# A four-layer decoder trunk on one core: stage boundaries with the last two output tiles in token halves, high terms first, and the second half's statistics between them

## The reference

```python
for i in range(DEPTH):
    ...
    hp = rmsnorm(xp, norm_g[i, 0])
    ...                                        # mp = mixer(hp), by i % 3
    xp = xp + rmsnorm(mp, norm_g[i, 1])
    ...
    xp = xp + rmsnorm(swiglu_ffn(rmsnorm(xp, norm_g[i, 2]), ffn_w1[i], ffn_w3[i], ffn_w2[i]), norm_g[i, 3])
```

## Time and profile before

| | us |
|---|---|
| median of three runs | 3369.45 |
| lowest and highest | 3368.85 and 3377.64 |
| the profiled execution | 3368.75 |
| its span in the trace | 3367.2 |

### The profile page before, as it was taken

One profiled execution on the slowest core, in us unless ns is written; L12 is line 12 of the kernel. 1 busy time (PEld: TensorE's weight loads), 2 busy tenths in 40 slices (PEclk: granted clock), 3 DMA queues, 4 the chain that ended last, 5 costly groups with the idle time before them and its releaser, 6 DMA issues.

```text
span 3367.2 us, 63399 instructions
## 1 busy us (share of the span) xinstructions
PE 3159.9 (94%) x26691; PEld 2913.2 (87%) x26691; DVE 1469.3 (44%) x2092; ACT 1078.8 (32%) x1529; POOL 170.6 (5%) x270
## 2 busy tenths in 40 slices
PE   7998999999999999899999899899999998899998
PEld 7986899999976666689999883789999896799998
DVE  3435644325460111254442599464432444554422
ACT  3413322222265444442222440432222332422222
POOL 1000100005000000010000100010000100100001
PEclk9998899999989999899999899899999898899999
DMA  4223223323205999822232220222332123222331
GB/s 112 82 63 107 69 87 87 101 76 78 79 29 203 362 390 389 296 70 87 87 98 84 62 69 0 64 71 87 87 99 76 57 75 111 71 82 87 94 95 45
DMA packets 472464, 368.12 MB, mean 109 GB/s; under 512 B 24745, under 2 KB 436830, under 8 KB 472316
## 3 DMA queue, kind: packets, MB, share of 16 engines
q1 hardware_dynamic: 459248, 349.25, 32.3%
q10 hardware_dynamic: 11020, 16.22, 1.4%
q0 software_dynamic: 2048, 0.53, 0.2%
HBM read 348.68 MB, written 17.26 MB: 109 GB/s over the span
## 4 chain that ended last, share of the span: by engine, by line
PE 80%; DVE 12%; ACT 4%; POOL 2%; issue 1%; ACTq 0%; POOLq 0%; DVEq 0%
PE acc L786 61%; PE acc L1274 3%; DVE big L2134 3%; PE acc L1243 2%; PE acc L1315 2%; PE acc L818 2%; DVE h_lo L1558 1%; POOL xT L766 1%; ACT mix L2567 1%; DVE wsp L1510 1%; DVE yT L1526 1%; PE acc L1047 1%; PE acc L1035 1%; DVE big L1586 1%; PE acc L1258 1%
## 5 line engine op out<-in xcount | busy, mean ns | idle before, releaser
L1510 DVE TENSOR_TENSOR wsp<-ring,wsp 128x1024 fp32r<-128x1024 f32 (+1 forms) x360 | 467.5, 1300 | 1122.9 <-ACT wsp L2217 1122.7
L786 PE MATMUL acc<-h_lo,wsp 128*128 128x272 f32 x4416 | 918.7, 290 | 0.0
L786 PE MATMUL acc<-h_hi,wsp 128*128 128x272 f32 x5376 | 897.6, 289 | 3.2 <-ACT rstd L2274 3.2
L2217 ACT ACTIVATE wsp<-ring 128x1024 fp32r<-128x1024 f32 (+1 forms) x360 | 401.6, 1117 | 1355.6 <-PE acc L786 1332.3
L786 PEld LDWEIGHTS acc<-h_hi,wsp 128*128 128x128 f32 x5376 | 758.9, 189 | 3.5 <-issue 3.5
L786 PEld LDWEIGHTS acc<-h_lo,wsp 128*128 128x128 f32 x4416 | 702.5, 191 | 0.0
L786 PE MATMUL acc<-i_hi,wsp 128*128 128x272 f32 x2560 | 440.4, 294 | 20.0 <-DVE wsp L1510 13.6
L786 PE MATMUL acc<-g_hi,wsp 128*128 128x272 f32 x2640 | 439.5, 288 | 0.0
L786 PEld LDWEIGHTS acc<-i_hi,wsp 128*128 128x128 f32 x2560 | 371.4, 194 | 22.8 <-issue 18.6
L786 PEld LDWEIGHTS acc<-g_hi,wsp 128*128 128x128 f32 x2640 | 371.7, 189 | 0.0
L786 PE MATMUL acc<-g_lo,wsp 128*128 128x272 f32 x1320 | 272.1, 288 | 0.0
(11 more groups left out here) (387 smaller groups left out, 3249.8 us busy)
## 6 DMA issues: line engine op xcount, KB each, us to landing
ring<-in_ffn_w SPq DMA_DIRECT2D x176, 512.0 KB, 3.9
mix<-in_cache_fox_v SPq DMA_DIRECT2D x96, 512.0 KB, 9.2
mix<-in_cache_fox_k SPq DMA_DIRECT2D x92, 512.0 KB, 8.8
ring<-in_ffn_w SPq DMA_DIRECT2D x64, 704.0 KB, 4.7
big<-in_cache_fox_k SPq DMA_DIRECT2D x32, 512.0 KB, 7.7
big<-in_cache_fox_v SPq DMA_DIRECT2D x32, 512.0 KB, 12.5
ring<-in_conv_w SPq DMA_DIRECT2D x24, 512.0 KB, 4.0
ring<-in_gla_wr SPq DMA_DIRECT2D x16, 512.0 KB, 4.0
```

The costliest lines, as they stand in the source:

```text
L786: last = pe.matmul(acc[:, bank + h, 0:HALF], wsp[:, s, w, k * P:(k + 1) * P], rhs[:, k0 + k, h * HALF:(h + 1) * HALF], start=start and k = ...
L1510: dve.tensor_tensor(wsp[:, s, 1, 0:tiles * P], ring[:, slot, 0:tiles * P], wsp[:, s, 0, 0:tiles * P], ALU.subtract).then_inc(wlo_done, 1)
L2217: act.activation(wsp[:, slot % SPLITS, 0, 0:tiles * P], ring[:, slot, 0:tiles * P], ACT.Copy)\
```

## The change

- The last two parts are computed half by half: for tokens 0 to 271 both parts, then for tokens 272 to 543 both. Behind a mixer the two parts are output tiles 6 and 7; in the ffn they are the two K blocks of tile 7. TensorE waits for the weights of both before the first.
- The column sums and the spread of half one stand inside the second half: the sums within its first part, the spread ahead of its second.
- Column sums and spread of half two go into the next stage's first tile, behind its first and its fourth high term.
- The first two tiles of a stage take all high terms (two products for each input tile) of both tiles, then the low terms of both, for half one, and then the same for half two.
- VectorE's order in `post` is new: the low part of the first weights goes behind three z of half one, and the z of half two alternate in pairs with the `h_lo` of half one. ScalarE makes the first two high parts of x early behind an ffn, and takes the root of half two behind the third.

```diff
@@ TensorE
-            def last_block(s, ktiles, k0, hi, lo, start, free):
+            def last_parts(parts, hi, lo, ready):
 
                 for h in range(2):
-                    for k in range(ktiles):
-                        if h == 1 and k == 4:
-                            pe.wait_ge(acc_out[4], free)
-                            column_sums(0)
...
+                    for i, (s, ktiles, k0, bank, first, last_one) in enumerate(parts):
+                        for k in range(ktiles):
+                            if h == 1 and i == 0 and k == 4:
+                                ready()
+                                column_sums(0)
+                            if h == 1 and i == 1 and k == 0:
+                                spread_half(0)
+                            for w, rhs in ((0, hi), (0, lo), (1, hi)):
+                                last = pe.matmul(acc[:, bank + h, 0:HALF], wsp[:, s, w, k * P:(k + 1) * P],
+                                                 rhs[:, k0 + k, HALVES[h]],
...
-            def post():
-
-                spread_half(0)
-                column_sums(1)
...
+            def second_sums(adds):
+
+                pe.wait_ge(acc_out[4], t.out[4])
+                column_sums(1, adds)
+                t.sum += adds
+
+            def second_spread():
+
                 spread_half(1)
                 t.out[4] += 1
...
+                for h in range(2):
+                    for j in range(2):
+                        if h == 0:
+                            pe.wait_ge(wlo_done, s0 + j + 1)
+                            pe.wait_ge(acc_out[2 * j], t.out[2 * j])
+                        for k in range(KD):
+                            if adds and h == 0 and j == 0:
+                                if k == 1:
+                                    second_sums(adds)
+                                if k == 4:
+                                    second_spread()
+                            high_terms(j, h, k)
+                    for j in range(2):
+                        last = low_terms(j, h)
+                        if h:
+                            last.then_inc(blk_done, 1)
...
                     else:
-                        last_block(j % SPLITS, KD, 0, o_hi, h_lo, True, o[4] + 2)
+                        pe.wait_ge(wlo_done, s0 + KD)
+                        pe.wait_ge(acc_out[6], o[6] + 1)
+                        t.early += 1
+                        last_parts(((0, KD, 0, 4, True, True), (1, KD, 0, 6, True, True)), o_hi, h_lo,
+                                   lambda: pe.wait_ge(early_out, t.early))
...
@@ VectorE
-                z_half(0, range(2))
+                z_half(0, range(3))
+                if mixer:
+                    dve.wait_ge(acc_out[4], t.out[4])
+                    add_square(squares, KD - 2, HALVES[1])
+                if weights:
+                    weights(0)
+                z_half(0, range(3, 5))
                 dve.wait_ge(last_sq, 2 * t.post + 2)
                 add_square(squares, KD - 1, HALVES[1])
-                z_half(0, range(2, 6))
+                z_half(0, range(5, KD))
                 dve.wait_ge(rcol_done, 2 * t.post + 2)
                 dve.reciprocal(rinv[:, 3:6], rcol[:, 3:6]).then_inc(rstd_done, 1)
-                z_half(0, range(6, KD))
-                between(1)
+                if lows:
+                    lows(0, range(2))
+                if weights:
+                    weights(1)
                 dve.wait_ge(spread_full, 2 * t.post + 2)
                 t.out[6] += 1
                 dve.wait_ge(acc_out[6], t.out[6])
-                z_half(1, range(2))
-                between(2)
-                z_half(1, range(2, KD))
+                for k in range(0, KD, 2):
+                    z_half(1, range(k, k + 2))
+                    if lows and k + 2 < KD:
+                        lows(0, range(k + 2, k + 4))
...
@@ ScalarE
+                if coming or mixer:
                     act.wait_ge(state_out, 16 * states[0])
                     high(0, KD, 16 * (t.blk // RING + 1), t.blk - 1)
...
+                if coming:
+                    for k in range(EARLY):
+                        high_half(*coming, 0, k)
+                act.wait_ge(blk_done, t.blk)
+                half_out(squares, bias, KD - 1, 1, last_sq, acc_out[6])
+                if coming or mixer:
+                    high(1, KD, 16 * (t.blk // RING + 1), t.blk)
...
+                        if early is not None and not h and k == 2:
+                            root_of(1)
+                            t.post += 1
```

More of the change, by code:

```diff
@@ L823, in post @@
-            def post():
-                spread_half(0)
-                column_sums(1)
+                    for i, (s, ktiles, k0, bank, first, last_one) in enumerate(parts):
[8 more added lines that the diff above has]
+                                                 rhs[:, k0 + k, HALVES[h]],
+                                                 start=first and k == 0 and w == 0 and rhs is hi,
+                                                 stop=last_one and k == ktiles - 1 and w == 1)
+                        last.then_inc(blk_done if h else half_done, 1)
@@ L827, in post, with stage_start, high_terms, low_terms @@
+            def second_sums(adds):
[3 more added lines that the diff above has]
+            def second_spread():
                 spread_half(1)
-                t.sum += KD
                 t.out[4] += 1
-            def stage_start(hi):
+            def stage_start(hi, adds=0):
                 s0 = t.split
-                def some(j, h, paced):
+                def high_terms(j, h, k):
+                    if j == 0:
+                        pe.wait_ge(hhi_done, t.hhi + h * KD + k + 1)
+                    for w in range(2):
+                        pe.matmul(acc[:, 2 * j + h, 0:HALF], wsp[:, j, w, k * P:(k + 1) * P], hi[:, k, HALVES[h]],
+                                  start=k == 0 and w == 0, stop=False)
+                def low_terms(j, h):
@@ L837, in some @@
                     for k in range(KD):
-                        if paced:
+                        if j == 0:
                             pe.wait_ge(h_done, t.h + h * KD + k + 1)
[L840 to L843, removed]
@@ L844, in some @@
-                    return last
[L846 to L851, removed]
+                        last = pe.matmul(acc[:, 2 * j + h, 0:HALF], wsp[:, j, 0, k * P:(k + 1) * P],
+                                         h_lo[:, k, HALVES[h]], start=False, stop=k == KD - 1)
@@ L883, in project_out @@
                 o, s0 = list(t.out), t.split
-                for m in range(KD):
+                for m in range(KD - 1):
                     it, j = divmod(m, RING)
@@ L1123, in ffn @@
                 o, s0 = list(t.out), t.split
-                for b in range(2 * KD):
+                for b in range(2 * KD - 1):
                     bank = b // 2 % 4 * 2
@@ L1511, in low, with post @@
                                   ALU.subtract).then_inc(wlo_done, 1)
-            def post(layer, which, squares, between):
-                dve.wait_ge(last_sq, 2 * t.post + 1)
-                add_square(squares, KD - 1, HALVES[0])
-                between(0)
-                dve.wait_ge(rcol_done, 2 * t.post + 1)
-                dve.reciprocal(rinv[:, 0:3], rcol[:, 0:3]).then_inc(rstd_done, 1)
-                dve.wait_ge(spread_full, 2 * t.post + 1)
-                dve.wait_ge(y_done, t.post + 1)
+            def post(layer, which, squares, mixer, weights=None, lows=None):
                 def z_half(h, tiles):
@@ L1618, in project_out @@
             def project_out():
-                for m in range(KD - 1):
-                    if m + 2 < KD:
-                        low((m + 2) % RING, KD, t.split + m + 3)
+                for m in range(KD - 2):
+                    low((m + 2) % RING, KD, t.split + m + 3)
                     bank = 2 * (m % 4)
@@ L2277, in project_out @@
             def project_out(bias=None):
-                for m in range(KD - 1):
-                    if m + 2 < KD:
-                        high((m + 2) % RING, KD, 16 * (t.blk // RING + (m + 2) // RING + 1), t.blk + m + 1)
+                for m in range(KD - 2):
+                    high((m + 2) % RING, KD, 16 * (t.blk // RING + (m + 2) // RING + 1), t.blk + m + 1)
                     act.wait_ge(blk_done, t.blk + m + 1)
```

147 lines of the change are left out of this document (83 added, 64 removed).

## The result

| | median us | lowest to highest | runs |
|---|---|---|---|
| before | 3371.03 | 3368.85 to 3377.64 | 4 |
| changed kernel | 3396.48 | 3395.82 to 3397.28 | 4 |

The ratio is 1.0067, 95% interval 1.0053 to 1.0082: the change costs 0.67%, about 23 us by the ratio and 25 by the medians. The profiled executions say 27.0 us (span 3394.2 against 3367.2).

What follows compares the result with a forecast made beforehand. TensorE's matmuls bound the kernel, VectorE and GpSimd together the boundaries after the first spread. 11.9 us without the clock, plus 14.8 half clock at stalls, minus 4.1 regained, gave +22.6 on 3368.75: 3391 us, range 3372 to 3408.

Steps and rivals of the forecast that it cites:

- Part 1: Before the halved last tiles, TensorE waits for split weights: 2.7 us behind mixers, 3.4 in ffns, four each, 24.6 us.
- Part 2: First spread at a boundary, now before the last block's second half: 0.3 us earlier behind a mixer, 0.7 in the ffn.
- Part 3: From first spread to first z of half two: 10.7 us instead of 9.4, +1.3 us at each of seven boundaries.
- Part 4: From first z of half two to the sums of squares: 12.55 us instead of 11.5, +1.05 us, from interleaving h_lo.
- The last boundary: After the final stage: a 2.2 us gap in GpSimd's additions against 0.7 gained by the earlier spread, +1.5 us.
- The clock at the stalls: TensorE's half clock behind the weight waits: 2.1 us lost at four ffn stalls, 1.6 behind four mixers, 14.8 us.
- the row of 3.00 us: Earlier trace's wait on split weights, followed by granted clock 0.50 from 1931.7 to 1936.9, 2.6 us lost.
- Rival (a): The clock holds at the weight stalls: +8 us, or +4, so 3373 to 3377 us; chance 0.14.
- the discount for h_lo that find GpSimd waiting: About one of six h_lo per boundary takes 0.42 us instead of 0.81: seven times -0.38, -2.7 us.
- the one that was to come back elsewhere, -4.1 us: Half clock behind the norm's sums costs 8.2 us; TensorE, coming later and waiting less, gets half back.
- Part 5: High terms first at a stage's start: same matmuls, worth nothing, because VectorE and GpSimd set the end.
- rival (b): Last tile's weights are split in time, so no stall shows: -17 us, 3352 us; chance 0.14.

Runs made afterwards that it cites:

- the two experiments on the wait: Early wait for the last block's split weights added to the kernel before: 3409.93 us; that wait moved behind the first half-block in the changed kernel: 3359.04 us.
- z first: Changed kernel with the weights wait moved later, and on VectorE all eight z of half two before the last six h_lo of half one: 3353.39 us, ratio 0.9944.
- the late wait: Changed kernel with the wait for the last block's split weights moved behind the first half of the block ahead of it: 3359.04 us, ratio 0.9957.
- low terms last: Later weights wait and all z of half two first, plus TensorE taking high terms of both halves before any low term: 3352.00 us, ratio 0.9938.

## Why the prediction was right

It gave 3391 us, +22.6 on the profiled execution; measured were 3396.5, with 27.0 us in the profiled executions. By its own steps:

- **Part 1, the new wait.** 24.6 us expected, 23.8 measured, eight times, at the place named. Shown from both sides by the two experiments on the wait.
- **Part 2, the first spread.** 12.5 us expected behind a mixer, 0.3 less than before. From the end of the block ahead of both parts (324.81) to the spread (337.26) the trace has 12.45, against 12.55 in the same stretch before: 0.1 less. In the ffn it has 17.95 twice, 19.05 and 18.93, with the half clock in it; less that loss it is 16.2, where 16.6 was expected.
- **Part 3, to the first z of half two.** 10.7 expected, 10.6 measured at the first boundary (337.26 to 347.89) and behind the ffns; the wait for the root in it is there (1.24 us). Behind the other three mixers it is 10.1 to 10.4. Over the seven boundaries +7.4 us, where 9.1 stood in the sum.
- **Part 4, to the sums.** 12.55 expected, 12.5 measured at six of the seven boundaries. That VectorE's order is the cause is shown by z first, which gives 11.1. But only two of the seven took 11.5 us before; four took 11.8 and one 12.5. Over the seven +6.4 us, where 7.35 stood in the sum.
- **The last boundary.** A gap of 2.2 us in GpSimd's additions expected ahead of half two; two gaps, 1.39 and 0.92, are there:

```profile
3368.50 3.69 POOL L768 TENSOR_TENSOR xT<-xT,yT 128x272 f32<-128x272 f32 x5 [399.89 <-DVE yT L1550]
3373.58 2.19 POOL L768 TENSOR_TENSOR xT<-xT,yT 128x272 f32<-128x272 f32 x3 [1.39 <-DVE yT L1550]
3376.69 5.76 POOL L768 TENSOR_TENSOR xT<-xT,yT 128x272 f32<-128x272 f32 x8 [0.92 <-DVE yT L1550]
```

- **The clock at the stalls.** 14.8 us expected as a mean over all; 12.1 measured, at two of four mixers and at all four ffn stalls, as the row of 3.00 us had it. Rival (a), the clock that holds, came true at two places of eight.

Set against the table, the sum has these parts. The path to the first spreads was forecast at +10.8 us (Part 2 with the clock at the stalls) and grew by 8.1. Parts 3 and 4 less the discount for h_lo that find GpSimd waiting were forecast at +13.8, and +13.8 was measured. That these agree is in part luck. The discount of 2.7 us was not earned: the pairs between the z take 1.74, 1.75 and 1.72 us at the first boundary, 0.87 each, since VectorE's z starts the next additions just as its h_lo begin. Parts 3 and 4 came out as much too high. The last boundary, from its first spread on, was forecast at +2.2 and grew by 2.5.

The term that was mis-sized is the one that was to come back elsewhere, -4.1 us; +2.6 was measured, and these 6.7 us are more than the whole distance between forecast and result. Behind the norm's sums its mechanism came true: two stretches at the half clock, 3.4 us at 786.8 and 6.8 at 2230.7, make 10.2 us against the 16.4 counted before, so about 3 us came back. They went again inside the stages, of which the sum says nothing. Of that, 1.7 us are longer stretches at the half clock, and the cause of the rest stays open; the table shows that the stages differ by as much between kernels that are the same there.

Part 5 took high terms first as worth nothing, where the experiment gives 8 us. In the sum this did not show, because parts 3 and 4 assumed throughout that TensorE would be ready when VectorE's sums are; with three products in turn and VectorE's new order it would not have been. The step was right for the changed kernel and wrong as the value of that edit. And rival (b), the case without the stalls, was forecast at -17 us; the late wait is that case made by an edit, and it gave -10.1 in the profile and 0.43% in the medians.

The prediction weighed a rule of the Trainium skill (SBUF — State Buffer, "SBUF: two separate sides"): the port pair that VectorE and GpSimd share is locked for a whole instruction, and not divided, when VectorE has two SBUF inputs. The trace agrees only in part. Beside h_lo, GpSimd's pairs of additions take 1.68 to 1.71 us, 0.85 each, while the h_lo take 0.87 each instead of the 0.42 to 0.5 that they take alone (eight in 3.99 us with GpSimd idle for all but the first). An estimate from these rows: taking strict turns, two h_lo of 0.42 and two additions of 0.80 would need 2.4 us, behind the 0.6 us that the first addition starts later than its z, 3.0 us a round. A round, from one pair of z to the next, is 2.5 us (347.89 to 350.38). VectorE alone would need 1.7. So the two hinder each other, but by less than a lock for the whole instruction would; the row decides again.

## What to carry to other kernels

Put a wait in front of the first instruction that needs it, not in front of the group: here the same wait 3 us later, behind work that needs only the first weights, turned +0.67% into -0.43% (behind a mixer; in the ffn it is 4 us later). Where a buffer has two slots and the order of use becomes A, B, A, B, ask when B's slot comes free before asking what the new order saves. Measure an edit in the stretch that it touches: there these kernels repeat to 0.1 us, while the rest of the program moves by several. And behind such a fix look at who is last: at these boundaries each gain on VectorE or GpSimd soon found TensorE, at the half clock from its own short waits, as the next bound.

The version with the late wait and all z first (ratio 0.9944), and the same with low terms last (0.9938), beat both the kernel before and the changed one. Which of the two is faster the medians do not settle; the boundaries alone are 3.8 us shorter with low terms last.

## What the runs showed of the hardware

- A stall of 2.67 us, the same at four places of one execution, left the clock at 1.00 at two of them and brought it to 0.50 for 3.4 us at the other two; one of 3.28 us brought it down at all four, for 3.4 to some 5.6 us of work. The price of such a wait was thus its length plus 0 to 2.8 us, and a mean over places is what could be forecast.
- One kernel's executions can differ by more than an edit is worth: with all z first, 3348.0 to 3357.0 us, at a mean granted clock of 0.970 and 0.968. These 0.2% are about 7 of the 9 us. The changed kernel stays within 1.5 us, at 0.963 in all four.
- The low part of the first weights took 1.79 us beside GpSimd's additions at the first boundary, where 1.43 stood in the earlier trace rows and 1.23 alone.
